# Matmuls of constants on TensorE's waits, in a two-block transformer kernel with routed experts

## What is computed

```python
def rms_norm(x, g):
    xf = x.astype(jnp.float32)
    y = xf * lax.rsqrt(jnp.mean(xf * xf, axis=-1, keepdims=True) + NORM_EPS)
    return (y * g.astype(jnp.float32)).astype(x.dtype)

    for layer in range(DEPTH):
        h = h + 0.5 * swiglu(rms_norm(h, ffn_norm[layer, 0]), ...)
        u = rms_norm(h, mix_norm[layer])
        ...
        h = h + mixed.astype(h.dtype)
        h = h + 0.5 * swiglu(rms_norm(h, ffn_norm[layer, 1]), ...)
    return rms_norm(h, final_norm)
```

## Time and profile before

| | |
|---|---|
| median of three runs | 3010.7 us (3009.11 to 3012.53) |
| profiled execution | 3008.26 us, span 3006.2 us |
| mean granted TensorE clock | 0.937 of full speed |
| TensorE busy | 2666.2 us, 89% of the span, 14137 matmuls |
| VectorE, ScalarE, GpSimd busy | 58%, 44%, 8% |
| DMA | 536.83 MB, mean 179 GB/s |

### The profile page before, as it was taken

One profiled execution on the slowest core, in us unless ns is written; L12 is line 12 of the kernel. 1 busy time (PEld: TensorE's weight loads), 2 busy tenths in 40 slices (PEclk: granted clock), 3 DMA queues, 4 the chain that ended last, 5 costly groups with the idle time before them and its releaser, 6 DMA issues. The chain is left out here.

```text
span 3006.2 us, 37401 instructions
## 1 busy us (share of the span) xinstructions
PE 2666.2 (89%) x14137; PEld 2056.4 (68%) x14137; DVE 1758.3 (58%) x2733; ACT 1318.9 (44%) x2065; POOL 253.4 (8%) x234
## 2 busy tenths in 40 slices
PE   6999886959999968998699988989799899788998
PEld 4666565847888846888533327878678788777786
DVE  3799878348999956455500016546555555457554
ACT  3223365238888844442210005435454444446443
POOL 1000046001111010024000000002000000110000
PEclk8999988969999978999799998999899999988999
DMA  6655500329996132230579984533145454420442
GB/s 272 224 205 219 193 1 1 112 95 347 413 413 268 50 140 75 108 113 1 193 296 411 411 323 167 198 135 118 57 159 205 150 186 173 155 100 16 185 179 77
DMA packets 94497, 536.83 MB, mean 179 GB/s; under 512 B 10864, under 2 KB 12272, under 8 KB 70640
## 3 DMA queue, kind: packets, MB, share of 16 engines
q1 hardware_dynamic: 87408, 509.45, 45.0%
q0 software_dynamic: 6768, 24.64, 2.2%
q10 hardware_dynamic: 144, 0.35, 0.0%
HBM read 599.94 MB, written 22.54 MB: 207 GB/s over the span
## 5 line engine op out<-in xcount | busy, mean ns | idle before, releaser
L1265 PE MATMUL ps<-w_hi,x_hi 128*128 128x512 f32 x1136 | 455.3, 401 | 13.5 <-DVE w_lo L2783 8.2
L1267 PE MATMUL ps<-w_hi,x_lo 128*128 128x512 f32 x1136 | 447.9, 394 | 0.0
L1266 PE MATMUL ps<-w_lo,x_hi 128*128 128x512 f32 x1136 | 447.6, 394 | 0.0
L1265 PEld LDWEIGHTS ps<-w_hi,x_hi 128*128 128x128 f32 x1136 | 217.1, 191 | 58.2 <-DVE w_lo L2783 8.7
L1267 PEld LDWEIGHTS ps<-w_hi,x_lo 128*128 128x128 f32 x1136 | 216.6, 191 | 47.1
L1266 PEld LDWEIGHTS ps<-w_lo,x_hi 128*128 128x128 f32 x1136 | 217.0, 191 | 43.7
L1265 PE MATMUL ps<-x_hi,w_hi 128*128 128x512 f32 (+1 forms) x512 | 204.6, 400 | 24.6 <-DVE x_lo L573 15.6
L1265 PE MATMUL ps<-w_hi,hidden_hi 128*128 128x512 f32 x536 | 210.8, 393 | 7.8 <-DVE hidden_lo L2950 6.0
L1267 PE MATMUL ps<-w_hi,hidden_lo 128*128 128x512 f32 x536 | 209.1, 390 | 0.0
L1266 PE MATMUL ps<-w_lo,hidden_hi 128*128 128x512 f32 x536 | 208.8, 390 | 0.0
L1267 PE MATMUL ps<-x_hi,w_lo 128*128 128x512 f32 (+1 forms) x512 | 197.8, 386 | 0.0
(11 more groups left out here) (716 smaller groups left out, 5763.0 us busy)
## 6 DMA issues: line engine op xcount, KB each, us to landing
weights_A<-in_moe_gate SPq DMA_DIRECT2D x132, 512.0 KB
weights_B<-in_moe_up SPq DMA_DIRECT2D x132, 512.0 KB
weights_A<-in_ffn_gu SPq DMA_DIRECT2D x24, 2048.0 KB, 7.9
weights_B<-in_ffn_gu SPq DMA_DIRECT2D x20, 2048.0 KB, 7.8
weights_C<-in_moe_down SPq DMA_DIRECT2D x66, 512.0 KB
weights_D<-in_moe_down SPq DMA_DIRECT2D x66, 512.0 KB
weights_C<-in_ffn_down SPq DMA_DIRECT2D x24, 1024.0 KB, 7.1
second_weights<-in_moe_gate SPq DMA_DIRECT2D x44, 512.0 KB
```

The costliest lines, as they stand in the source:

```text
L1265: nc.tensor.matmul(out, w_hi, x_hi, start=first, stop=False)
L1266: nc.tensor.matmul(out, w_hi, x_lo, start=False, stop=False)
L1267: return nc.tensor.matmul(out, w_lo, x_hi, start=False, stop=last)
```

## The change

A helper `stay_awake(bank, n)` issues n float32 matmuls of the identity with itself, 128 columns, into a PSUM bank that nobody reads at that moment. It is called at twelve places in TensorE's lists. They signal nothing. At two places a wait stands in front that TensorE would have come to later anyhow in `turn_hidden` (`who_done`), and at one a wait that it did not have (`first_added`).

```diff
+    def stay_awake(self, bank, n):
+        for _ in range(n):
+            self.nc.tensor.matmul(self.ps[:, bank, 0:P], self.c("ident"), self.c("ident"), start=True, stop=True)
 rms_norm, after the sums of squares:
+                    self.stay_awake(3, 2)
                     pe.wait_ge(s["copied"], 1)
...
                     last.then_inc(s["spread"], 1)
+                    self.stay_awake(3, 20)
 out_projection, first on TensorE:
+                    self.stay_awake(7, 10)
 experts and expert_pairs:
+                    pe.wait_ge(s["who_done"], 1)
+                    self.stay_awake(RB, 14)
                     turn_x(0)
 expert_pairs, last on TensorE:
+                    pe.wait_ge(s["first_added"], nt)
+                    self.stay_awake(HB, 12)
 odd_in, first on TensorE:
+                    self.stay_awake(7, 7)
 head_norm_gate:
                     last.then_inc(s["totals"], 1)
+                    self.stay_awake(6, 8)
                     for j in range(pairs):
                         pe.wait_ge(s["diag_made"], j + 1)
...
                         last.then_inc(s["spread"], 1)
+                    self.stay_awake(6, 5)
 norm_turned, first on TensorE:
+                    self.stay_awake(7, 14)
 row_projection, first on TensorE:
+                    self.stay_awake(7, 10)
 feed_forward, last on TensorE:
+                    self.stay_awake(0, 9)
```

## The result

The changed kernel takes 2987.73 us (median, 2985.41 to 2989.06), and 2987.98 us when measured again beside the second experiments; the kernel before took 3011.61 and 3009.57 us on the same occasions. The ratios are 0.9928 [0.9913, 0.9943] and 0.9931 [0.9917, 0.9945], thus -23.9 and -21.6 us by the medians. The forecast was 3001.7 us with 2993 as its lower end. Its sign was right, its size 2.4 to 2.7 times too small.

What follows compares the result with a forecast made beforehand. TensorE was taken as the bound, nearly fully used but with its clock often low after waits. Terms summed to -9.0 us: 3008.3 to 2999.3, and with the median 2.4 us above, 3001.7 us; range 2993 to 3009.

Steps and rivals of the forecast that it cites:

- the rival in which constants do nothing: Whole kernel: clock does not heed constants multiplied with mostly zeros, calls fit the waits; 0 to +4, 3012 us, chance 0.04.
- the forecast's +1.9: Head norm with four pairs: 8 matmuls in a gap of 1.49 us take 3.4 us if low, harm +1.9.
- first norm and output projection: First norm into out-projection: 4.4 us of low products, best -2.1, harm +1.3, taken -2.0 us.
- odd projection: Third norm into odd_in: 4.7 us low, best -2.3, harm 0.8, taken -0.6 us.
- The norm on 256 tokens: The 20 matmuls make the barrier 0.6 to 4.6 us late; ends 0 and +4.0, taken +1.3 us.
- then what I take, since the pauses that are left still cost some of it: All sites: each term gives best gain, harm with added matmuls low, then a taken value, since remaining pauses cost some gain.
- Row projections: Two row projections: 5.2 and 4.7 us low, best -4.9 for both, harm +1.3 each, taken -2.8 us.
- Experts' first rows: Experts' gathered rows: 4.6 us low and a transpose of 8; best -2.9, harm +0.3, taken -1.2 us.
- Pairs' first rows: Pairs' gathered rows: best -2.5, but the 14 end 2 to 5 us before the rows; taken -0.4, harm 0.
- Turned norms: Two turned norms: 32 instructions take 5.3 and 5.7 us against 3.7 high; best -3.6, harm +1.6 each, taken -3.3.
- rival 3: Whole kernel: clock holds through the short pauses left, two thirds of the best sum comes; -17, 2994 us, chance 0.11.
- The Trainium skill's rule that I had weighed: Gathered rows: by the rule, real transposes give the clock back, gather terms nothing or positive; the forecast counted transposes as work.

Runs made afterwards that it cites:

- the second experiments: Occasion that remeasured the kernel before and the changed kernel, both unchanged (ratio 0.9931), and ran the changed kernel with 8 for 20 matmuls behind the norm's spread: 2985.70 us.
- the late calls: Changed kernel with only the calls of row projections, turned norms and feed-forward's end kept: 3000.86 us, 0.9974 of the kernel before.
- the five calls: Changed kernel with only the calls of both gathers, row projections, turned norms and the feed-forward's end kept: 2992.32 us, 0.9944 of the kernel before.
- the two of 20: 20 matmuls each at the start of first projection and scan, added to the changed kernel along with 16 behind each routing's counting: 2995.79 us.
- the four further calls: Changed kernel plus 20 matmuls at the start of first projection and of scan, and 16 behind the counting of each routing: 2995.79 us, 0.9959 of the kernel before.

## Why the prediction fell short

**Right:** what bounds the kernel; the two prices of an added matmul's instruction (0.11 and 0.21 us; 20 take 2.47 us at clock 1.00, and the low ones 0.22 to 0.24 us each); that such work raises the clock, against the rival in which constants do nothing; and the sign. The late spread in the head norm came as worked out, and the spread itself is faster:

```profile
1411.46 6.99 PE L2650 MATMUL ps<-constants,head_squares 128*128 128x2 f32 x32 [2.26 <-ACT head_squares L2640]
1418.30 3.76 PE L475 MATMUL ps<-constants 128*128 128x128 f32 x16
...
1421.86 4.45 PE L2657 MATMUL ps<-head_rstd_diagonal,constants 128*128 128x128 f32 x32
```

L2657 starts 10.40 us after L2650 where it was 8.47: 1.9 us late, the forecast's +1.9, and takes 4.45 us where it took 6.57. Taken -0.3 with its projection, stages 47.9 to 47.7. Likewise first norm and output projection (taken -2.0; 111.7 to 110.4 on average), odd projection (-0.6; -0.8), head norm with attention (-0.2; -0.1), pairs' end and first feed-forward (+0.4; 0.0), the second and third feed-forward (0; 397.1 to 397.2 in the three traces before, 397.0 and 397.4 after).

**The norm on 256 tokens** (taken +1.3) moved between both ends. VectorE's and ScalarE's scaling and the call, in the first and then in the second trace of the changed kernel:

```profile
1463.83 4.63 PE L475 MATMUL ps<-constants 128*128 128x128 f32 x40
...
1464.55 3.30 ACT L425 ACTIVATE normed<-normed,modulation 128x256 f32<-128x256 f32 x8 [1.99 <-DVE normed L468]
```
```profile
1470.45 5.66 PE L475 MATMUL ps<-constants 128*128 128x128 f32 x40
...
1471.21 3.30 ACT L425 ACTIVATE normed<-normed,modulation 128x256 f32<-128x256 f32 x8 [2.50 <-DVE normed L468]
```

The barrier is late by 1463.83 + 4.63 - 1467.85 = 0.6 us in one and 1.6 us in the other, and by 3.0 us in the trace with the norms' calls alone, where the stage took 14.8 us. Against 10.6 before, 12.0 us is +1.4 on average.

**The failed step: "then what I take, since the pauses that are left still cost some of it".** Four terms were taken below their best ends and a fifth was put at nothing; in the traces of the changed kernel the stages reached those ends or passed them:
- Row projections: taken -2.8, best -4.9; 59.0 to 54.2, -4.8.
- Experts' first rows: taken -1.2, best -2.9. "The call starts low and rises late" was half right: its clock is 0.63, but it has risen when the rows come, and L1487 behind it waits only 0.21 us for the DMA. The part from the rows on is the call's: 16.9 us in seven of the eight traces that have it, 18.7 to 19.2 in all that don't. The routing ahead of it is in part luck: it took 36.6 and 39.5 us in the changed kernel and 40.3 to 40.5 before, but also 37.6 in the kernel with only the pairs' call, where none stands ahead of it. So of the stages' -3 to -6 us, 2 to 3 are the call's.
- Pairs' first rows: taken -0.4, best -2.5; the stage took 3.4 us less in the changed kernel on average, and 1.8 less with this call alone. I had set the call's end at "2 to 5 us before the rows arrive"; in the first trace it takes 6.08 us at clock 0.53, thus nearly all low, and the rows' transposes begin 0.74 us after it:

```profile
1492.77 6.08 PE L475 MATMUL ps<-constants 128*128 128x128 f32 x28 [0.26 <-DVE token_of_row L2209]
1499.59 1.09 PE L2005 MATMUL ps<-constants,tile_rows 128*128 128x128 f32 x8 [0.74 <-DMA tile_rows<-h_tok,token_of_row]
```

- Turned norms: taken -3.3, best -3.6; 23.1 to 19.2, -3.8.
- The projections behind the turned norms: no term at all. 193.3 to 190.3, -2.9.

By the stages of these two traces the terms were -4.5 where I took -1.2, -3.4 for -0.4, -4.8 for -2.8, -3.8 for -3.3 and -2.9 for 0: 11.7 us more than taken, and -9.0 - 11.7 = -20.7 us. That this meets the measured change so well is partly luck. Over all nineteen traces with 128-column constants, those with a site's call against those without, the same five make -2.8, -1.8, -4.4, -3.7 and -1.8, some 14.4 us. Row projections (54.2 us in every trace with the call) and turned norms (19.2 to 19.5) are sure; the projections behind the turned norms (189.8 to 195.4 with the calls) and both routings scatter by more than they gain. So the five terms were 7 to 12 us too small, which is half to nearly all of the miss of 13 to 15; the rest is in no single term.

The wrong idea was the discount itself, that the pauses left would take back part of each site's gain. In the site's own stage they did not, not even with one call alone: both row projections took 27.1 us, both turned norms 9.62, the experts' rows 16.9, as in the full change. Low stretches come and go in the stages around, and which pause they come from no run tells. The measured time is nearest to rival 3 ("More", 2994 us, two thirds of the best sum), with nine tenths of the best sum in place of two thirds; but the odd projection and attention, through whose pauses it let the clock hold, still begin partly low.

The Trainium skill's rule that I had weighed: the real transposes of L1487 and L2005 run in 1.09 us for 8, the high price, against 1.97 before. Behind L1487 the first products have clock 1.00. Behind L2005 they do not in the first trace of the changed kernel:

```profile
1501.90:1505.30 3.40, 3.35 (x8) 0.51 0.49 152
```

In the second trace they start high, with clock 1.00 over 1509.52 to 1513.00 us. The Trainium skill (TensorE: Matmul & The Clock Gate, Part 4) says that the full clock does not engage for transposes in the PE's transpose mode. The experts' stretch does not agree with it; the pairs' in the first trace could, but there pauses of 0.74 and 1.26 us stand around the transposes as well, and no run parts the two. By the kernels' times each gather was worth some 3 us, and not nothing.

**Open:** whether both gathers together (10.5 us) give more than the two alone (6.3), or whether that is the width of the interval. Whether sites need one another: 7.8 us for the late calls against 1.8 for their parts speaks for it, with intervals that touch, and the traces' lengths speak against it. What the full change gains beyond the five calls' 16.8 us. Why the turned norms alone are worth 0.9 us [-3.6, +1.8] when their trace shows 3.8 us in the norms and 2.4 in the projections behind, and no stage behind them that is longer. The stages ahead of all calls: up to the first row projection the kernel with that call alone has the code of the kernel before, yet its trace took 2162.1 us against 2156.3, 2148.7 and 2153.1; the first stage alone took 492.4 to 493.4 us in the three traces before and 494.7 and 495.3 in the changed kernel's two, with the same code. The length of the program does not decide it: with one call of 14 the same stage took 492.6 us when it was the pairs' and 495.2 when it was the experts', both behind it in time. Chance is the nearest explanation; no kernel was traced often enough to show it. And which low stretch in which stage comes from which pause, since no run moved a single pause by a known amount.

## What to carry to other kernels

Where a product-bound stage begins behind an idle TensorE, constants multiplied in the wait can be worth half the low stretch. Put them in the wait itself, and read from the trace on which side of the barrier it lies. The calls of the row projections and turned norms stand first in their stages, where TensorE waits for its first data anyhow, and they pay; the two of 20 also stood first in their stages, but there most or all of the wait was over by the barrier, and together they cost 6 to 7 us. There the place is the end of the stage before, behind the last result that others need. Use 128 columns (2 cost 17 us here), and let the last one end as the awaited data comes. Judge such a change as a whole, by medians: alone a site showed its stages 4.8 us shorter and the kernel 0.9 us faster, and one trace moves by 1.3 to 3 us in stages that nothing touched.

## What the hardware showed unexpectedly

A float32 instruction of 2 columns took 0.22 us at granted clock 0.51, as much as one of 128 columns at the low level; the 128-column form in its place took 0.12, at 1.00. The narrow constant is thus no cheap one. One call that is the same in every trace can leave the clock at either level behind it: the 28 instructions ahead of the pairs' rows took 6.08 us in one trace of the changed kernel and 4.71 in the other. And the mean granted clock is no measure of the gain: with the four further calls it was 0.955, that of the changed kernel, at 8 us more.
